# Two-layer trunk with 32-expert MoE on one Trainium2 core: the gate and up products of an expert taken apart

## The reference

```python
D_MODEL, SEQ, DEPTH, N_EXPERTS, EXPERT_TOPK, D_EXPERT = 1024, 256, 2, 32, 2, 512

for i in range(DEPTH):
    h = h + mixer(rms_norm(h, g_mix[i]))          # convolution, then attention
    h = h + hier_moe(rms_norm(h, g_ffn[i]), ...)
    gate = sigmoid(rms_norm(h, g_ple[i]) @ ple_w_gate[i])
    h = h + gate * (p[i] @ ple_w_proj[i])

# hier_moe: every token goes to 2 of 32 experts; of expert e, for its tokens xblk:
    h = jax.nn.silu(xblk @ w_gate[e]) * (xblk @ w_up[e])    # 1024 -> 512
    return h @ w_down[e]                                     # 512 -> 1024
```

## Time and profile before

| | us |
|---|---|
| median of 3 runs | 1335.97 |
| the profiled execution, its own time | 1336.18 |
| span of the profiled execution | 1334.1 |
| PE busy | 1035.9 (78%) |
| POOL, DVE, ACT busy | 453.5, 316.9, 302.5 |
| experts of layer 0, first gate-and-up product to last scatter | 160.5 to 602.5 |
| experts of layer 1 | 849.8 to 1292.6 |

### The profile page before, as it was taken

One profiled execution on the slowest core, in us unless ns is written; L12 is line 12 of the kernel. 1 busy time (PEld: TensorE's weight loads), 2 busy tenths in 40 slices (PEclk: granted clock), 3 DMA queues, 4 the chain that ended last, 5 costly groups with the idle time before them and its releaser, 6 DMA issues.

```text
span 1334.1 us, 27871 instructions
## 1 busy us (share of the span) xinstructions
PE 1035.9 (78%) x10412; PEld 591.8 (44%) x10413; DVE 316.9 (24%) x886; ACT 302.5 (23%) x710; POOL 453.5 (34%) x743
## 2 busy tenths in 40 slices
PE   6968877667777776778998889787777777777678
PEld 5744544333444333334454555443333444334443
DVE  3994300000120000005136771210000121001111
ACT  5873311111111111112113561211111111112121
POOL 2340164443455334330000130454344354343520
PEclk9989988888889888888999699898888889889989
DMA  9952399999999999998415503699999999999980
GB/s 304 380 193 65 117 400 428 429 428 429 428 429 428 429 427 430 427 419 318 132 63 188 254 25 153 253 400 426 431 426 430 426 430 427 430 427 421 429 357 31
DMA packets 62872, 449.24 MB, mean 337 GB/s; under 512 B 10841, under 2 KB 21713, under 8 KB 38256
## 3 DMA queue, kind: packets, MB, share of 16 engines
q1 hardware_dynamic: 57776, 448.25, 81.2%
q10 hardware_dynamic: 5056, 0.48, 0.3%
HBM read 447.66 MB, written 1.05 MB: 336 GB/s over the span
## 4 chain that ended last, share of the span: by engine, by line
DMA 44%; PE 39%; DVE 9%; issue 4%; ACT 3%; SPq 1%; POOL 0%; ACTq 0%; DVEq 0%
DMA ring<-in_moe_w_up 43%; PE PS L560 15%; PE PS L445 10%; PE PS L539 2%; PE PS L575 2%; ACT arena L1131 1%; PE PS L547 1%; PE PS L582 1%; DVE hn L1399 1%; PE PS L433 1%; PE PS L729 1%; DVE arena L1399 1%; DVE ppw L1742 1%; SPq L318 1%; PE PS L600 1%
## 5 line engine op out<-in xcount | busy, mean ns | idle before, releaser
L560 PE MATMUL PS<-ring,arena 128*32 128x256 f32 x4160 | 334.5, 486 | 190.5 <-DMA ring<-in_moe_w_up 166.2
L560 PEld LDWEIGHTS PS<-ring,arena 128*32 128x32 f32 x4160 | 161.5, 134 | 355.3 <-issue 218.2
L1451 DVE TENSOR_TENSOR arena<-PS,arena 64x256 f32<-64x256 f32 x65 | 27.8, 428 | 590.9 <-ACT arena L1195 585.1
L575 PE MATMUL PS<-ring,arena 128*32 128x256 f32 x2080 | 125.7, 381 | 30.8 <-DVE arena L1454 30.8
L1195 ACT ACTIVATE arena<-PS 64x256 f32<-64x256 f32 x64 | 24.2, 377 | 515.6 <-PE PS L560 515.6
L966 POOL TENSOR_SCALAR arena<-arena 128x32 f32<-128x32 f32 x64 | 18.9, 295 | 291.3 <-PE PS L547 285.8
L925 POOL TENSOR_SCALAR arena<-arena 128x512 f32<-128x512 f32 x67 | 105.7, 1578 | 24.8 <-POOL arena L972 12.9
L575 PEld LDWEIGHTS PS<-ring,arena 128*32 128x32 f32 x2080 | 73.1, 109 | 61.1 <-issue 37.4
L919 POOL TENSOR_SCALAR arena<-arena 128x32 f32<-128x32 f32 x260 | 88.7, 364 | 13.1 <-POOL arena L966 12.9
L927 POOL TENSOR_TENSOR arena<-arena 128x512 f32<-128x512 f32 x67 | 85.6, 1278 | 5.6
L582 PE MATMUL PS<-arena 32*128 32x256 f32 x1040 | 74.5, 397 | 6.6 <-ACT arena L1193 0.6
(11 more groups left out here) (323 smaller groups left out, 1209.5 us busy)
## 6 DMA issues: line engine op xcount, KB each, us to landing
ring<-in_moe_w_gate SPq DMA_DIRECT2D x62, 2048.0 KB, 17.9
ring<-in_moe_w_up SPq DMA_DIRECT2D x62, 2048.0 KB, 22.3
ring<-in_moe_w_down SPq DMA_DIRECT2D x62, 2048.0 KB, 24.0
wb<-in_ple_w_gate SPq DMA_DIRECT2D x4, 2048.0 KB, 32.5
ring<-in_conv_w_pw SPq DMA_DIRECT2D x3, 2048.0 KB, 19.0
ring<-in_nsa_w_in SPq DMA_DIRECT2D x3, 2048.0 KB, 15.0
wb<-in_moe_w_gate SPq DMA_DIRECT2D x2, 2048.0 KB, 14.7
wb<-in_moe_w_up SPq DMA_DIRECT2D x2, 2048.0 KB, 13.2
```

What stands on the lines that cost most here:

```text
L560: i = pe.matmul(PS[32 * j:32 * j + 32, BGU, 0:256].rearrange("q (p c) -> q p c", c=2), xT[:, k, :], w[:, k, :].rearrange("q (p h c) -> q h ...
L575: i = pe.matmul(PS[32 * j:32 * j + 32, BY, 0:Q4], hT[:, c, 32 * f:32 * f + 32], w_dn(s)[:, f, c, Q4 * j:Q4 * (j + 1)], start=(q == 0), sto ...
L1451: return v.tensor_tensor(hh[64:128, :], PS[64:128, BGU, 0:256], gs[64:128, :], ALU.mult)
```

## The change

Gate and up become two products. Each uses all four strips, strip j computing a quarter of the 512 outputs: element j of every four, 128 columns a product, so `quarters` issues 32 products of 128 columns for gate and 32 for up. Gate lies in bank `BGU`, up in bank `BHT`; silu, their product `hh` and its transpose are one piece of 128 x 128, and the transpose goes to the second quarter of `BGU`. Gate and up loads have a semaphore each (`gate_w`, `up_w`), PE waits for each before its own product, and SP refills gate's place when the gate product is done (`g_mm`) and up's when the up product is (`gu_mm`). DVE waits for silu and for the up product. Some semaphores of the attention layer are merged (`c1_x`, `c1_g` into `c1_d` and so on), with the same order; these hunks are left out below.

```diff
             def expert(L, e, s, used=None, held=None):
-                if used is not None:
-                    sp.wait_ge(gu_mm, used)
                 for g in range(2):
+                    if used is not None:
+                        sp.wait_ge((g_mm, gu_mm)[g], used)
                     if held != g:
-                        gate_up_load(L, e, ring[:, s, 4096 * g:4096 * (g + 1)], g, gu_in[s])
+                        gate_up_load(L, e, ring[:, s, 4096 * g:4096 * (g + 1)], g, (gate_w, up_w)[g][s])
...
-            def gate_up(s, xT):
+            def quarters(w, xT, bank):
                 for k in range(8):
                     for j in range(4):
-                        w = w_gu(s)[:, j // 2, :, :]
-                        i = pe.matmul(PS[32 * j:32 * j + 32, BGU, 0:256].rearrange("q (p c) -> q p c", c=2), xT[:, k, :],
-                                      w[:, k, :].rearrange("q (p h c) -> q h p c", h=2, c=2)[:, j % 2],
-                                      start=(k == 0), stop=(k == 7))
+                        i = pe.matmul(PS[32 * j:32 * j + 32, bank, 0:P], xT[:, k, :],
+                                      w[:, k, :].rearrange("q (p j) -> q j p", j=4)[:, j], start=(k == 0), stop=(k == 7))
                 return i
+
+            def gate(s, xT):
+                return quarters(w_gu(s)[:, 0, :, :], xT, BGU)
+
+            def up(s, xT):
+                return quarters(w_gu(s)[:, 1, :, :], xT, BHT)
 
             def h_T():
                 pe.sem_inc(pe_step, 1)
-                for c in range(2):
-                    i = pe.transpose(PS[:, BHT, 64 * c:64 * (c + 1)], hh[64:128, c::2], ident[64:128, 64:128])
-                return i
+                return pe.transpose(PS[:, BGU, P:2 * P], hh, ident[:, :])
...
-                    pe.wait_ge(gu_in[s], ld * 2)
+                    pe.wait_ge(gate_w[s], ld)
                     pe.wait_ge(xgT_ok, gi - 1)
-                    gate_up(s, xgT).then_inc(gu_mm, 1)
+                    gate(s, xgT).then_inc(g_mm, 1)
+                    pe.wait_ge(up_w[s], ld)
+                    pe.wait_ge(row_dve, L + 1)
+                    up(s, xgT).then_inc(gu_mm, 1)
...
-                        act.wait_ge(gu_mm, n)
-                        nc.scalar.activation(gs[64:128, :], PS[0:64, BGU, 0:256], ACT.Silu).then_inc(sil_ok, 1)
+                        act.wait_ge(g_mm, n)
+                        nc.scalar.activation(gs, PS[:, BGU, 0:P], ACT.Silu).then_inc(sil_ok, 1)
...
             def hmul():
-                return v.tensor_tensor(hh[64:128, :], PS[64:128, BGU, 0:256], gs[64:128, :], ALU.mult)
+                return v.tensor_tensor(hh, PS[:, BHT, 0:P], gs, ALU.mult)
...
                     dve.wait_ge(sil_ok, n)
+                    dve.wait_ge(gu_mm, n)
                     hmul().then_inc(h_ok, 1)
```

More of the change, by code:

```diff
@@ L139, in build @@
         xfree[1] = off[0]
-        gs = carve(256)
-        hh = carve(256)
-        hT = carve(128).rearrange("p (c s) -> p c s", c=2)
+        gs = carve(128)
+        hh = carve(128)
+        hT = carve(128)
         ysb = carve(256)
@@ L266, in build @@
         in_in = [sem(f"in_in{i}") for i in range(5)]
-        gu_in = [sem(f"gu_in{i}") for i in range(2)]
+        gate_w = [sem(f"gate_w{i}") for i in range(2)]
+        up_w = [sem(f"up_w{i}") for i in range(2)]
         held_in = sem("held_in")
@@ L298, in build @@
         s_sclv = sem("s_sclv")
-        c1_mm, c1_x, c1_s, c1_g, c1_t, c1_T, kc_mm, kc_x, kct_mm, kcT_ok, vcr_ok = [
-            sem(s) for s in ("c1_mm", "c1_x", "c1_s", "c1_g", "c1_t", "c1_T", "kc_mm", "kc_x", "kct_mm",
+        c1_mm, c1_d, c1_a, kc_mm, kc_x, kcT_ok, vcr_ok = [
+            sem(s) for s in ("c1_mm", "c1_d", "c1_a", "kc_mm", "kc_x",
                              "kcT_ok", "vcr_ok")]
         qt_mm, qt_act = sem("qt_mm"), sem("qt_act")
-        sc_mm, sc_d, sc_e, sc_p, sct_mm, pct_ok = (sem("sc_mm"), sem("sc_d"), sem("sc_e"), sem("sc_p"),
-                                                   sem("sct_mm"), sem("pct_ok"))
+        sc_mm, sc_d, sc_e, pct_ok = sem("sc_mm"), sem("sc_d"), sem("sc_e"), sem("pct_ok")
         s_mm, s_max, s_exp, s_fac, s_scl, t_mm, pt_dve, pt_act, o_mm, o_ok = [
@@ L390, in _ @@
             for n, b in ((4, R0[1]), (0, R0[2]), (2, WB[2])):
+                if n == 4:
+                    sp.wait_ge(gu_mm, NE - 1)
                 if n == 0:
@@ L574, in down @@
                     for j in range(4):
-                        i = pe.matmul(PS[32 * j:32 * j + 32, BY, 0:Q4], hT[:, c, 32 * f:32 * f + 32],
+                        i = pe.matmul(PS[32 * j:32 * j + 32, BY, 0:Q4], hT[:, 32 * q:32 * q + 32],
                                       w_dn(s)[:, f, c, Q4 * j:Q4 * (j + 1)], start=(q == 0), stop=(q == 3))
@@ L661, in one_expert @@
                             pe.wait_ge(X["x_xgT"], c)
-                            pe.wait_ge(gu_in[s], ld * 2)
-                            gate_up(s, xxgT).then_inc(X["x_gu"], 1)
+                            pe.wait_ge(gate_w[s], ld)
+                            gate(s, xxgT).then_inc(X["x_g"], 1)
+                            pe.wait_ge(up_w[s], ld)
+                            up(s, xxgT).then_inc(X["x_gu"], 1)
                             pe.wait_ge(X["x_h"], c)
@@ L799, in _ @@
             pe.wait_ge(kc_x, 2)
-            pe.transpose(PS[:, 0, 384:444], kcx[0:60, 2:4, :], ident[0:60, 0:60]).then_inc(kct_mm, 1)
+            pe.transpose(PS[:, 0, 384:444], kcx[0:60, 2:4, :], ident[0:60, 0:60]).then_inc(kc_mm, 1)
             def scores(hp):
@@ L857, in _ @@
             scores(2)
-            pe.wait_ge(sc_p, 1)
+            pe.wait_ge(sc_d, 3)
             for t in range(NT):
@@ L1261, in _ @@
                 nc.scalar.copy(qT[:, 2 * b:2 * b + 2, :], PS[:, 2 + b, :].rearrange("p (k q) -> p k q", k=2)).then_inc(qt_act, 1)
-            act.wait_ge(c1_t, 1)
-            nc.scalar.copy(h1T, PS[:, 1, 0:256].rearrange("p (c n) -> p c n", c=2)).then_inc(c1_T, 1)
+            act.wait_ge(c1_mm, 2)
+            nc.scalar.copy(h1T, PS[:, 1, 0:256].rearrange("p (c n) -> p c n", c=2)).then_inc(c1_a, 1)
             kT_copy(2, 7)
```

56 lines of the change are left out of this document (29 added, 27 removed).

## The result

| | median us | range | runs |
|---|---|---|---|
| before | 1335.26 | 1333.56 to 1336.41 | 4 |
| after | 1372.20 | 1370.51 to 1377.32 | 4 |

Ratio 1.0291, 95% interval 1.0266 to 1.0317. The forecast was 1336.2 with a range of 1331 to 1349: both missed. Rival 1, slow single-element reads, named the mechanism and priced it at 1350, 22 us short.

What follows compares the result with a forecast made beforehand. The prediction took loaded bytes (DMA at 428 GB/s) to bound mid-layer, leaving only starts, ends and a dip: +3.7 + 1.2 - 2.4 - 1.9 - 0.5 = +0.1 on 1336.18, so 1336.2 us, range 1331 to 1349.

Steps and rivals of the forecast that it cites:

- Rival 1: Gate and up products: single-element reads are slow, 60 ns a record, 1350 us (1343 at 45 ns); chance 0.18.
- the record's duration: Gate and up products: a record of 128 columns takes 34 ns at full clock, bounds 31 and 60.
- the sum: Whole kernel: layer starts +3.7 and +1.2, ends -2.4 and -1.9, dip -0.5, together +0.1 us.
- the starts: First experts of each layer: +3.7 and +1.2 us in the sum; Rival 1 adds +1.7, +4 and +3.
- the overflow pass: Layer 1's extra pass: the sum has -0.5 us for the dip behind it, Rival 1 +3.5.
- the ends: Last down product of each layer starts +5.0 to +5.2 us after the up load: -2.4 and -1.9 us.
- The code stalls: First experts' products wait for program blocks; layer 0 loses +2.6 to +5.0 us, taken +3.7.
- Layer 1's term: Start of layer 1: gate load behind expert 1's product goes out 0 to +3.4 us later, taken +1.2.
- Rival 2: Layer starts and ends: code comes in time, so earlier releases pay -9.4 us: 1327, half of it 1331; chance 0.24.
- Rival 3: Starts and ends: late code, +5.0 and +3.4 us, and cold-clock ends, -0.4 and 0: 1343.7; chance 0.10.
- rival 4: Expert loop: its code no longer stays on the engine and is fetched again, near 1,950 us; chance 0.08.
- At nothing: Each expert: reshaped silu, multiply, copy, single transpose and added DVE and SP waits cost no time.

Runs made afterwards that it cites:

- e1: Changed kernel with each strip reading 128 adjacent columns in place of every fourth one; 1339.67 us, ratio 1.0055 to the kernel before.
- e2: Changed kernel with each strip reading pairs of neighbouring columns, two of every four, over half the columns; 1337.93 us, ratio 1.0041 to the kernel before.
- e12: Changed kernel with each strip reading every second column of its half in place of every fourth; 1337.20 us, ratio 1.0024 to the kernel before.
- e3: Kernel before, its 256-column products reading every fourth element alone over two matrix rows; 1375.23 us, ratio 1.0318 to the kernel before.
- e13: Changed kernel reading adjacent pairs, loads split, four 64x64 products for the transpose, overflow product of the kernel before; 1330.71 us, ratio 0.9971.
- e14: e13 with only the gate load's release joined again, so that it waits for the up product; 1338.24 us, ratio 1.0030 to the kernel before.
- e5: Kernel before with two never-run extra products per overflow branch, 512 instructions more in the loop; 1354.26 us, ratio 1.0157.
- e6: Kernel before with three never-run extra products per overflow branch, 768 instructions more in the loop; 2064.92 us, ratio 1.5478.

## Why the prediction was wrong

**The step that failed: the record's duration.** "I take 34" between bounds of 31 and 60 ns. It is 59; e1, e2, e12 and e3 show that the reads alone make it so. The argument given for 34 was the nearest row in columns, but the one property in dispute, single elements, no row had. With ends that far apart and a stated rule on the side of the upper one, 0.18 was too little for it.

**The rival's price failed too, and that is why even the range missed.** It said that PE's work of 14.1 us an expert stays under 14.7 and "decides mid-layer only once a record passes 65 ns". The 14.1 were nearly right (13.96 measured), what they were compared with was not: 14.7 us is the time of three loads, but the held matrices and the first experts' loads were there beforehand. What an expert took before, over 30 experts, was 416.48/30 = 13.88 us, so PE becomes the bound at 13.9 us and not at 14.7. The bound in the middle of a stretch is the mean over the stretch, not the period of one expert. With nothing left to spare, whatever holds PE up counts in full. Rival 1, with the sum's own terms, priced the starts at +13.6, and up to expert 2's product they cost 16.0. It priced the overflow pass at +3.5, and that cost some 16. It priced the ends at -2.9, and they cost +4.0: the last expert's loads are in, and its whole product of 7.6 us stands behind the expert before.

**The code stalls were right in place and too small in size.** After breaks at record 32 of expert 0 (35 forecast) and 13 of expert 1 (16 forecast), q8 has 27 packets, the loop stays on the engine. e1, whose records are those the sum had assumed, missed the sum of +0.1: +7.3 by the ratio, +3.0 by the traces. In its trace the gate load behind expert 1's product goes out at 186.94, in a run that began its experts 0.93 us earlier than that of the earlier trace rows: +7.1 where the sum had +3.7 and the upper bound was +5.0. In e2, with the same records, it is +5.3 (186.11, begun 0.06 later). The first three lines are e1's, the other two e2's:

```profile
162.74 5.09 PE L562 MATMUL PS<-ring,arena 128*32 128x128 f32 x96 [1.27 <-issue]
183.57 5.46 PE L562 MATMUL PS<-ring,arena 128*32 128x128 f32 x114 [4.63 <-issue]
186.94 0.33 SPq L319 DMA_DIRECT2D ring<-in_moe_w_gate  x1
...
163.17 2.97 PE L562 MATMUL PS<-ring,arena 128*32 128x128 f32 x96 [1.53 <-issue]
186.11 0.33 SPq L319 DMA_DIRECT2D ring<-in_moe_w_gate  x1
```

The 2 us between them are the clock: in e1 it was low before expert 0's product began (0.50 granted in 154 to 164) and its 96 records took 5.09 us, 53 ns each; in e2 it was full (1.00 in 163.2 to 166.1) and they took 2.97, 31 ns each. What is left, +5.3, is just over the bound: expert 1's second break ends at 182.74 in e2, within the 180.6 to 183.0 forecast, and the rest of gate behind it takes 3.4 us where the sum had 2.6. Layer 1's term was right (+1.7 against 1.2 in e1: 877.10 for 872.12, less the 3.3 us by which layer 0's last down product came later). The ends were right: the down product starts 5.25 and 5.06 us after the last up load in e1, -2.3 and -2.0 for -2.4 and -1.9.

**Rival 2 was half true.** The release pays 7.5 us (e13 against e14), near the 9.4 of its full form; the waits' 3.3 are the sum's 4.3 at the ends. But its condition, code that comes in time, did not hold: the longer program takes back more than that, up to the 21 us of e5. The two nearly cancel in e1, e2 and e12 (+3 to +7 by the ratio), so "no change" would have been nearly right had the reads been fast, as a balance of two terms and in part by luck. Rival 3's total (1343.7) is near e1's (+7.3 by the ratio), but not its terms: the ends did not turn out cold.

**The range.** By the prediction's own chances more lay outside 1331 to 1349 than the 0.2 that it states; half of rival 2 (0.12), rival 4 (0.08) and the full form of rival 1 are nearly 0.3.

**At nothing, rightly:** silu, multiply, copy, the added waits. No trace shows PE waiting longer for them: the idle before the down product is 0.47 us, as before.

## What to carry to other kernels

Where the sum rests on a pattern that no row shows, give the end a stated rule speaks for the larger chance, and compute when an engine becomes the bound from the mean period of the whole stretch. Before spending an engine's spare time, list what it hides: here a pass that comes once had cost nothing and then cost some 16 us. Lengthening a loop is a cost of its own even in branches that never run: count the blocks that a first pass meets, and shorten rare branches before hot ones. A split load pays at starts and ends only, and there by the time that the engine takes when it is slow.

## What was not expected of the hardware

- A TensorE record in float32 takes 0.23 to 0.24 ns a column with two wanted elements to 16 bytes and 0.46 ns with one, in four strips at full clock (28.9 to 30.6 against 58.7 ns for 128 columns, 60 against 117 for 256).
- A block of code that is only asked for takes a place, by the prediction's count of blocks: 8 blocks stay at 1354 us (e5), 9 make 2065 (e6), with seven of them run in both.
- At its lower clock the old product of 256 columns is not twice as long, as the part ahead of the prediction says: 6.63 us in layer 1 of e5 (0.51 granted in 860 to 866) for 3.86 at full clock, 1.7 times.
- With the down matrix, a third of the bytes, in pieces of 4 KB in place of 16 KB, the rate in mid-layer falls from 428 to 420 GB/s.
- What stays open: how the 21 us of e5 divide between the program's length and its second jump; and whether slow reads go by lines of 16 bytes or by the distance between elements.
